# Two neighbouring rows of an expert's weights per partition, read from activations with a step of two

## The reference

```python
logits = t @ router_w + router_b                 # (tokens, 32)
top_v, top_i = lax.top_k(logits, 4); gates = softmax(top_v)
for each expert e, for its tokens xb (rows of t):
    a = xb @ w_gate[e] + b_gate[e]               # w_gate[e]: 1024 x 1024, float32
    u = xb @ w_up[e] + b_up[e]
    hid = min(a, 7) * sigmoid(1.702 * min(a, 7)) * (clip(u, -7, 7) + 1)
    yb = (hid @ w_down[e] + b_down[e]) * gate    # w_down[e]: 1024 x 1024, float32
out = sum over a token's four experts
```

## Time and profile before

| | us |
|---|---|
| three runs | 1183.87, 1180.65, 1183.45 (median 1183.45) |
| the profiled execution, first to last instruction (its span) | 1177.5 |
| TensorE busy | 1100.9 (93%) |
| TensorE weight loads busy (beside the matmuls) | 541.2 |
| VectorE busy | 231.0 (20%) |
| ScalarE busy | 126.4 (11%) |
| mean granted TensorE clock | 0.976 |
| moved by DMA | 426.96 MB, 363 GB/s over the span |

### The profile page before, as it was taken

How to read it: one execution, slowest core, us unless ns; L and a number is a source line. 1 busy time by engine, 2 the same in 40 slices (tenths; PEclk the granted TensorE clock), 3 DMA queues, 4 the chain that set the end, 5 groups by cost and what they waited for, 6 DMA issues and landing times.

```text
span 1177.5 us, 13748 instructions
## 1 busy us (share of the span) xinstructions
PE 1100.9 (93%) x5600; PEld 541.2 (46%) x5600; DVE 231.0 (20%) x528; ACT 126.4 (11%) x250; POOL 30.7 (3%) x37
## 2 busy tenths in 40 slices
PE   7999998999999999999999999999999999999995
PEld 5787756344444444444444444444444444344431
DVE  4422463111110111111111111111111111111114
ACT  2231321000000000000000000000000000000001
POOL 0220011000000000000000000000000000000000
PEclk9989998899999999999999999999999999999998
DMA  8974454899999999999999999999999999999980
GB/s 264 354 265 144 144 203 177 331 388 410 409 409 409 409 409 410 410 410 410 410 410 410 410 410 410 410 410 410 410 410 410 410 410 410 410 409 409 409 321 36
DMA packets 127392, 426.96 MB, mean 363 GB/s; under 512 B 10537, under 2 KB 27026, under 8 KB 127362
## 3 DMA queue, kind: packets, MB, share of 16 engines
q1 hardware_dynamic: 125234, 423.83, 91.9%
q10 hardware_dynamic: 2128, 2.70, 0.9%
HBM read 425.46 MB, written 1.05 MB: 362 GB/s over the span
## 4 chain that ended last, share of the span: by engine, by line
PE 88%; DVE 7%; issue 3%; ACT 2%; DMA 0%; SPq 0%; DVEq 0%
PE bank L948 38%; PE bank L981 20%; PE bank L924 10%; PE bank L931 3%; PE bank L649 3%; PE bank L851 2%; DVE arena L1290 2%; DVE arena L1285 2%; PE bank L972 2%; DVE arena L1287 2%; PE bank L942 2%; PE bank L837 1%; PE bank L789 1%; PE bank L725 1%; PE bank L607 1%
## 5 line engine op out<-in xcount | busy, mean ns | idle before, releaser
L948 PE MATMUL bank<-ring,arena 128*64 128x512 f32 x2016 | 445.3, 593 | 0.0
L948 PEld LDWEIGHTS bank<-ring,arena 128*64 128x64 f32 x2016 | 154.8, 137 | 257.3 <-issue 253.3
L981 PE MATMUL bank<-ring,arena 128*64 128x512 f32 x1024 | 239.5, 622 | 24.3 <-issue 19.1
L981 PEld LDWEIGHTS bank<-ring,arena 128*64 128x64 f32 x1024 | 85.7, 142 | 157.6 <-issue 157.6
L924 PEld LDWEIGHTS bank<-arena 128*128 128x128 f32 x1024 | 119.7, 196 | 25.3 <-issue 25.3
L924 PE MATMUL bank<-arena 128*128 128x64 f32 x1024 | 124.1, 281 | 0.0
L1285 DVE TENSOR_SCALAR arena<-bank 128x512 f32<-128x512 f32 x32 | 22.1, 692 | 356.8 <-PE bank L948 356.8
L1294 DVE COPY arena<-bank 128x512 f32<-128x512 f32 x32 | 22.1, 692 | 291.7 <-PE bank L981 291.7
L568 ACT ACTIVATE arena<-arena 128x512 f32<-128x512 f32 x32 | 20.1, 630 | 491.8 <-DVE arena L1281 491.8
L931 PE MATMUL bank<-arena 64*128 64x512 f32 x256 | 72.0, 640 | 0.8 <-DVE arena L1294 0.8
L1281 DVE TENSOR_SCALAR arena<-bank 128x512 f32<-128x512 f32 x32 | 22.1, 692 | 185.4 <-PE bank L948 185.4
(11 more groups left out here) (242 smaller groups left out, 533.9 us busy)
## 6 DMA issues: line engine op xcount, KB each, us to landing
ring<-in_moe_w_up SPq DMA_DIRECT2D x128, 1024.0 KB, 17.0
ring<-in_moe_w_down SPq DMA_DIRECT2D x128, 1024.0 KB, 14.5
ring<-in_moe_w_gate SPq DMA_DIRECT2D x124, 1024.0 KB, 13.5
ring<-in_w_in SPq DMA_DIRECT2D x12, 1024.0 KB, 12.0
ring<-in_w_out SPq DMA_DIRECT2D x4, 1024.0 KB, 12.7
arena<-in_moe_w_gate SPq DMA_DIRECT2D x4, 1024.0 KB, 4.8
arena<-in_x SPq DMA_DIRECT2D x2, 512.0 KB, 4.6
arena<-in_ln_in_g SPq DMA_DIRECT2D x1, 512.0 KB, 9.6
```

The lines of the kernel that those rows point to most:

```text
L948: ins = mm(b[h * SL:(h + 1) * SL, :], xT[par][:, kt, :], unit_at(4 * m + q)[:, k, h * 512:(h + 1) * 512], start=False, stop=kt == KT - 1)
L981: ins = mm(bank[6][h * SL:(h + 1) * SL, :], hidT[:, kt % 4, (kt // 4) * SL:(kt // 4 + 1) * SL], unit_at(8 + q)[:, k, h * 512:(h + 1) * 512 ...
```

## The change

`unit_src` now reads unit q so that partition p gets rows 256q+2p and 256q+2p+1, which lie side by side in HBM: one run of 8 KB per partition. The unit is the same 1 MB of HBM and lands in the same slot; the destination is given as one row of 2048 values. To match, slice kt = 2q+h of `xT` and `hidT` must hold channels 256q+2p+h. So the two places that make them read their stationary operand with a step of two values: the gather's block of `xh`, and the transposes' block of `u_c` (`pair_rows`). The biases, the selection, the outputs and the width and count of all matmuls stay. No instruction is added, removed or moved on any engine; the order on all of them is word for word the same but for the shape of the weights' DMAs (128x2048 in place of 128x2x1024).

```diff
         def unit_src(e, u):
             m = (w_gate, w_up, w_down)[u // (UPE // 3)]
             q = u % (UPE // 3)
-            return m[0, e].rearrange("(k p) n -> p k n", p=P)[:, 2 * q:2 * q + 2, :] if isinstance(e, int) else \
-                m[0, bass.ds(e, 1)].rearrange("a (k p) n -> p (a k) n", p=P)[:, 2 * q:2 * q + 2, :]
+            rows = slice(q * 2 * P, (q + 1) * 2 * P)
+            return m[0, e, rows, :].rearrange("(p k) n -> p (k n)", k=2) if isinstance(e, int) else \
+                m[0, bass.ds(e, 1), rows, :].rearrange("a (p k) n -> p (a k n)", k=2)
...
+        def unit_dst(v):
+            return v.rearrange("p k n -> p (k n)")
+
+        def pair_rows(v, kt):
+
+            return v.rearrange("p (q s k) -> p q k s", s=P, k=2)[:, kt // 2, kt % 2, :]
...
-                sp.dma_start(spare[q], unit_src(NE - UNROLL, q)).then_inc(spare_in, 16)
+                sp.dma_start(unit_dst(spare[q]), unit_src(NE - UNROLL, q)).then_inc(spare_in, 16)
...
-                    sp.dma_start(slot(at % RING), unit_src(it * UNROLL + i // UPE, i % UPE)).then_inc(landed[at % RING], 16)
+                    sp.dma_start(ring[:, at % RING, :], unit_src(it * UNROLL + i // UPE, i % UPE)).then_inc(landed[at % RING], 16)
...
-                        ins = mm(bank[7][:, kt * SL:(kt + 1) * SL], xh[:, t, kt * P:(kt + 1) * P], sel[:, par, t, :], start=t == 0, stop=t == 1)
+                        ins = mm(bank[7][:, kt * SL:(kt + 1) * SL], pair_rows(xh[:, t, :], kt), sel[:, par, t, :], start=t == 0, stop=t == 1)
...
-                    ins = tr(bank[7][:, c * P:(c + 1) * P], u_c[:, c * P:(c + 1) * P], ident[:, :])
+                    ins = tr(bank[7][:, c * P:(c + 1) * P], pair_rows(u_c, c), ident[:, :])
```

More of the change, by code:

```diff
@@ L342, in _ @@
                     for u in range(UPE):
-                        sp.dma_start(slot(u), unit_src(e, u)).then_inc(landed[u], 16)
+                        sp.dma_start(ring[:, u, :], unit_src(e, u)).then_inc(landed[u], 16)
             for t in range(NT):
```

## The result

The changed kernel takes 1194.61 us (median of 4 runs, 1194.05 to 1196.24) against 1183.66 of before (4 runs): 1.0108 times as long, 95% interval 1.0086 to 1.0129. The forecast of 1183 with "no measurable change" as the likeliest case was wrong. The time lies within the range 1177 to 1196, but on the side that had 0.23.

What follows compares the result with a forecast made beforehand. The prediction took TensorE to bound the expert stage, with DMA close behind. Transfers, gather and transposes summed as 0 + 0 + 0 on a span of 1177.5 us; with the runs' median 5.95 above it, 1183, range 1177 to 1196.

Steps and rivals of the forecast that it cites:

- no measurable change: Whole kernel: likeliest case, chance 0.70, at 1183 us, own range 1179 to 1187 by the clock's events.
- the side that had 0.23: Whole kernel: the chance given to a measurably slower time, beside 0.64 for same and 0.13 for faster.
- the transfers' gain: Expert stage's weight units: 409 to at best 421 GB/s, but 0 on the path, since TensorE waits for no unit.
- The clock's term: Down products slowed by the lower clock, 1.7 us each: about ±4 us for one execution, less for a median.
- parts 2 and 3 of the sum: Stepped weight loads in gather (0 to 122 us) and transposes (0 to 14 us); both taken as 0.
- a gather of 4 us or more: Gather of each expert: the sign that would put the step on the path; 3.7 us expected if right.
- The far end: Gather and transposes: 136 us in all if a step of two halves the rate of the weight loads.
- the first at the lower clock +6.7: First gather, run with the clock at 0.53: doubled by the step at worst, +6.7 us within the gather's 122.
- A stepped load pays for its lines: Rival, gather and transposes of every expert: full price 136 us (1319), a tenth of it 1197; chance 0.15.
- partial range of 1190 to 1210: Whole kernel's time if stepped loads pay only part of their full price; half of that rival's 0.15.
- Makes transfers slower: Rival, ring's weight transfers: the new layout slows them; 5% slower costs 26 us, 1209; chance 0.06.
- doesn't do what it says: Rival, weight transfers: packets stay at 4 KB, time 1183 as well; its chance lies within the 0.70 for no change.

Runs made afterwards that it cites:

- e1: The kernel before with the new transfers alone (8 KB runs), gather and transposes reading contiguous columns; 1183.14 us, 1.0017 times before.
- e2: The kernel before with the step of two in the gather's weight loads alone, old transfers; 1188.74 us, 1.006 times before.
- e3: The kernel before with the step of two in the four transposes alone, old transfers; 1189.83 us, 1.0097 times before.
- f1: The kernel before with one unread product of 512 float32 columns in each of TensorE's two idle places per expert; 1173.18 us, 0.9948 times before.
- f2: The changed kernel with one unread product of 512 float32 columns in each of TensorE's two idle places per expert; 1180.84 us, 1.0012 times before.
- g4: The kernel before with the four transposes done four times over (16), at a step of four; one run, mean clock 0.986, no time given.
- e4: The kernel before with both stepped reads (gather and transposes) and the old transfers; 1195.15 us, 1.0117 times before.
- f3: The kernel before with a step of four values in gather and transposes; 1405.6 us (two runs).

## Why the prediction was wrong

**Right:** that TensorE and not DMA bounds the expert stage, that the transfers' gain would be 0 on the path, and the sizes there: 421 GB/s estimated, 422 measured; 49,152 packets fewer, 127,392 to 78,240. e1 shows the 0 by itself. The clock's term was named too, with 1.7 us an event.

**The step that failed** is the choice of the lower end for parts 2 and 3 of the sum: "The nearest rows are those of the moving operand", and from them "I take 0". I took the rate at which the moving operand is read (9.4 bytes/ns, 1.7 ns per 16 bytes) as one that the weight loads could reach as well. They reach 1.83 ns a piece, 8.7 bytes/ns. The stepped load needs 1.75 to keep its pace (112 ns for 64), so it misses by 5%: 6 ns on each of 32 loads, 0.20 us a gather, 6.2 us over 31. The margin was thinner than I wrote, too. The 8.8 bytes/ns come from 116 ns, the whole gather divided by its 32 loads; from load to load it is 112 ns, so 9.1 against 9.4, a margin of 3% and not 7%. Borrowed from another operand, it was too thin to carry a forecast of exactly 0. The transposes' 0.09 us, 2.9 us over 32, are more than four times 6 ns, so the price of pieces does not explain that part; it was set to 0 by the same argument, and its cause is open. The prediction had written down that 3% on these loads could be measured, and gave the case 0.15. Its sign for it, a gather of 4 us or more, was set too high: 3.91 was enough.

The far end had a wrong term: "the first at the lower clock +6.7". The first gather takes 6.93 us at a step of two as at a step of one, since the clock is what limits it there.

**The rivals.** "A stepped load pays for its lines" was the right mechanism with its price mis-sized: it named a tenth to the whole of 136 us, and the measured loads cost 9.0, a fifteenth. The measured 1194.61 lies in its partial range of 1190 to 1210, in part because the clock added to the 9.0. "Makes transfers slower" and "doesn't do what it says" did not occur.

**The clock** was written down as luck, the same for both kernels. e2 agrees with that; e3 doesn't: with 2.3 us more at equal clock its runs are 9 us longer on average, so a change in the stretch where TensorE waits can shift how often the clock falls. Of the 10.95 us between the medians, 9.2 are left at equal clock. The other 1.75 are the clock's, and whether the change or luck set them is not shown. f1 and f2 show that filling the stretch's two idle places takes the slow products away between 230 and 1150 us; g4 shows that they can also be gone with both places left idle.

## What to carry to other kernels

Before paying on the engine that bounds a kernel to make a faster stream for one that doesn't, read the lead of the data over its reader: here it was 11 us at its thinnest, so a 3% faster DMA could bring nothing, while 6 ns on each of a thousand weight loads and 0.09 us on each expert's transposes cost 0.8%. Where weight loads set the pace (narrow moving operands), keep the stationary float32 operand contiguous; a step of two is nearly free and not quite, a step of four doubles the load, if the clock is at its upper level. And where a kernel's runs scatter by more than an edit is worth, compare at equal granted clock, per kernel and by the trace's start-to-start times; then look whether filling TensorE's short waits takes the scatter away.

## What the runs showed of the hardware

- A gather's weight load of 128 float32 columns took 112 ns or about 1.83 ns per 16-byte piece touched, whichever is longer (steps of 1, 2, 3, 4, 8), the same beside 410 GB/s of DMA writes and beside 6 (steps of 2 and 4). At half the clock the first of the two became 213 ns and the second stayed (213 ns at steps of 1, 2, 3; 233 at 4; 238 at 8).
- The load of a transpose went at 120 to 122 ns with a step of four, over 16 in a row; with none, in groups of four, the last two distances were about 110.
- Packets of 8 KB took 309 to 321 ns on one DMA engine, those of 4 KB 159 to 172: 422 against 409 GB/s on the core.
- With two idle places of 0.85 and 0.73 us per expert of 30 us, the granted clock fell to its lower level (1.2 GHz) for some 3.4 us in 2 to 11 experts after the first (profiled executions of e1, before, after, e2, e3, e4), and runs of one kernel lay up to 21 us apart. With both places filled (f1, f2), and with twelve more transposes between them (g4), it fell in none between 230 and 1150 us. In f3, with slower gathers, all down products but the last were slow, at a mean clock of 0.876.
